# Mixer slots of a two-layer decoder trunk: other PSUM banks for the second S5 input half, and attention items spread over four column tiles

## The chip, the cores and the metric

The kernel runs as one program on 1 core of one Trainium2 chip. The metric is the device time of one execution in microseconds. Before the change it is 2696.19 us, the median of 3 runs (2693.93 to 2703.63).

## What is computed

A trunk of two layers over one sequence of 256 tokens, width 2048, all in float32. Each layer has a mixer and a gated MLP with a short causal convolution. In the mixer one projection of the normalised input feeds three groups of heads:

```
h = rmsnorm(x, g_pre_mix) * (1 + sc1) + sh1          # sh, sc, gt from silu(c) @ w_ada + b_ada
proj = h @ w_in                                      # 41 column tiles of 128 in the kernel
y_m = mlstm_group(qk, v, o, i, f)                    # gated linear attention, 2 chunks of 128
y_s = s5_group(u)                                    # complex diagonal state, scan over tokens
y_n = nsa_group(q, k_cmp, v_cmp, k_slc, v_slc, ...)  # attention of three kinds, gated sum
x = x + gt1 * rmsnorm(concat(y_m, y_s, y_n) @ w_out, g_post_mix)
```

In the attention group, for each of 2 key heads (4 query heads each), each of 2 query blocks of 128 and each of 3 kinds (compressed keys, selected blocks, window), a softmax over the keys is weighted by a gate and summed: 12 items in all. With 256 tokens every block is selected, so the second and third kind are plain causal attention over 128 or 256 keys.

## The kernel before, in words

**Split precision.** Every weight chunk (128 x 1024 f32) is loaded into one of 5 ring slots by SyncE's queue, copied to `w_hi` by ScalarE (`w_head`, L1038), and its rest is written to `w_lo` by VectorE (`w_rest`, through L1406). TensorE multiplies with both. A ring slot is loaded again when VectorE has taken the rest of the chunk in it. Small S5 and compression weights ("raw" chunks) go through the same ring and are freed by the matmuls that use them. SyncE issues the loads strictly in order.

**Column tiles.** The mixer's input projection takes 41 column tiles in the order: 4 of S5 input u (tiles 0 to 3), 12 of keys and values (4 to 15), 1 of gates (16), 8 of queries (17 to 24), 8 of mLSTM q/k (25 to 32), 4 of mLSTM v (33 to 36), 4 of mLSTM o (37 to 40). A tile is 48 matmuls (`proj`, L616) over two weight chunks. Each engine has its own loop over tiles, written by hand, in which all the smaller work of the mixer is placed at a fixed tile number:
- TensorE, tile n: `proj(n)`, then the small matmuls of that tile (`s5_in` L715, `s5_out` L730/L733, `v_tokens` L770, `scores` L803/L808, `weights_t` L825/L827, `weighted_sum` L839/L842, `reduce_unit` L590).
- ScalarE, slot n: `w_head(2n+4)`, which needs the first half of tile n done by TensorE, `in_tile(n)` (evacuates the tile), `w_head(2n+5)`, then `s5_gelu` L1178, the evacuation of `v_tokens` L1260, `weights_out` L1197/L1199, `exps` L1186, `heads_out` L1205. After a slot the next `w_head` follows.
- VectorE, slot k: `w_rest(2k+4)`, for tiles 25 to 32 the mLSTM convolution (`qk_conv`, three operations), `w_rest(2k+5)`, `masked` (scale, mask and row maximum), two or three chunks of the adaLN product in layer 0 and one or two in layer 1 (`ada_chunk`, L1412), a piece of the S5 scan in slots 19 to 24 (`s5_scan`), `weighted` (L1737 and two or three L1406).

**An attention item before.** Item j, with `ITEM_TILE` = 27: `scores(j)` on TensorE in tile 27+j; in the same slot `masked(j)` on VectorE, `exps(j)` on ScalarE, and at the end of the slot `weighted(j)` on VectorE; `weights_t(j)` (transposes) on TensorE in tile 28+j, `weights_out(j)` on ScalarE, and `weighted_sum(j)` on TensorE in tile 29+j. `scores(j)` waits for `masked(j-1)`, since all scores use PSUM banks 2 and 3. Items 4, 5, 10 and 11 have 4 x 256 scores a row, items 1, 2, 7 and 8 have 4 x 128, the others 4 x 15.

**S5 before.** Both halves of the S5 input product go to PSUM banks 2 and 3. TensorE's first matmul of the second half (tile 20) therefore waits for `s5_bv(1)`, which VectorE gives after reading the first half (`s5_scan(0, 0)`, slot 19). `s5_out(1, ...)` (tiles 25 to 27) writes bank 5, `reduce_unit` bank 7 (tiles 23, 29 and 36 in layer 0, tile 29 in layer 1).

**Gate row.** At the end of slot 33 VectorE computes the gate gain; ScalarE sends it to memory (L1077), and in slot 34 waits for it to have landed before it issues the read back (L1082). After tile 40 the mLSTM part and the output projection follow.

Of the kernel before, what the change touches and what calls it, by code (L numbers as in the profile page):

```python
# [165 lines left out]
def trunk(nc, x, c_cols, pos, consts, aux_d, ada_d, ada_b, glu_d, stream, out):  # L166
    with ExitStack() as ctx:
# [408 lines left out]
        def _(pe):  # L576
# [82 lines left out]
            for l in range(DEPTH):  # L659
# [45 lines left out]
                def s5_in(h, part):  # L705

                    n = R_IN + 2 * h + part
                    raw_full(l, n)
                    if h == 0 and part == 0:
                        s5_tr_ev.wait(pe, l, UT)  # L710
                        s5_u.wait(pe, l, 1)
                    if h == 1:
                        s5_bv.wait(pe, l, 1)
                    for j in range(SH):
                        m = pe.matmul(ps[:, 2 + part, j * SN:(j + 1) * SN], raw(n)[:, j * P:(j + 1) * P],  # L715
                                      s5_u2[:, SH * h + j, :], start=True, stop=True)
                    raw_used.by(m)

                def s5_out(h, part):
# [5 lines left out]
                    if h == 1 and part == 0:  # L725
                        ch_g.wait(pe, l, 2)
# [65 lines left out]
                def scores(n):  # L792
                    g, qt, kind = ITEMS[n]
                    if n:
                        ns_m.wait(pe, l, n)
                    else:
                        s5_bv.wait(pe, l, 2)
                        cc_ev.wait(pe, l, 2)
                        rp_d.wait(pe, l, 7)
                    for h in range(GQ):  # L800
                        q = mix[:, T_Q + GQ * g + h, qt * P:(qt + 1) * P]
                        if kind == 0:
                            m = pe.matmul(ps[:, 2, h * 16:h * 16 + NC], q, kcT[:, g * NC:(g + 1) * NC],  # L803
                                          start=True, stop=True)
                        else:
                            kt = (T_KS if kind == 1 else T_KW) + g
                            nk = (qt + 1) * P
                            m = pe.matmul(ps[:, 2 + h // 2, (h % 2) * SEQ:(h % 2) * SEQ + nk], q, mix[:, kt, 0:nk],  # L808
                                          start=True, stop=True)
                    ns_s.by(m)  # L810
# [35 lines left out]
                for n, t in enumerate(ORDER):  # L846
# [22 lines left out]
                    if n == ITEM_TILE - 2:  # L869
                        v_tokens(0)  # L870
                    if n == ITEM_TILE:
                        v_tokens(1)
                    if 0 <= n - ITEM_TILE < NI:
                        scores(n - ITEM_TILE)
                    if 0 <= n - ITEM_TILE - 1 < NI:
                        weights_t(n - ITEM_TILE - 1)
                    if 0 <= n - ITEM_TILE - 2 < NI:
                        weighted_sum(n - ITEM_TILE - 2)
                    if n in ADA_TILE[l]:
                        u = U_IN[l] + ADA_TILE[l].index(n)  # L880
                        sg_ev.wait(pe, l, 1)
# [134 lines left out]
        def _(s):  # L1016
# [13 lines left out]
            for l in range(DEPTH):  # L1030
# [177 lines left out]
                for n in range(NT):  # L1208
# [47 lines left out]
                    if n in (ITEM_TILE - 2, ITEM_TILE):  # L1256
                        a = (n - ITEM_TILE + 2) // 2
# [3 lines left out]
                    if 0 <= n - ITEM_TILE - 1 < NI:  # L1261
                        weights_out(n - ITEM_TILE - 1)
                    if 0 <= n - ITEM_TILE < NI:
                        exps(n - ITEM_TILE)
                    if n - ITEM_TILE - 2 in (2, 5, 8, 11):
                        heads_out(n - ITEM_TILE - 2)
                    if n == ITEM_TILE + 1:
# [4 lines left out]
                    if n == ITEM_TILE + 4:  # L1272
# [131 lines left out]
        def _(v):  # L1404
# [75 lines left out]
            for l in range(DEPTH):  # L1480
# [167 lines left out]
                def s5_scan(h, piece):  # L1648
# [4 lines left out]
                    re_, im_ = ps[:, 2, :], ps[:, 3, :]  # L1653
# [94 lines left out]
                for k in range(NT):  # L1748
# [3 lines left out]
                    if k < NT - 1:  # L1752
                        w_rest(2 * k + AHEAD + 1)
                    if 0 <= k - ITEM_TILE < NI:
# [25 lines left out]
                    if 0 <= k - ITEM_TILE < NI:  # L1780
                        weighted(k - ITEM_TILE)
                    if k == ITEM_TILE + 2:
# [160 lines left out]
ITEM_TILE = 27  # L1943
# [130 lines left out]
```

## Time and profile before

| | |
|---|---|
| median of 3 runs | 2696.19 us |
| profiled execution, its own time | 2703.81 us |
| its span | 2702.0 us |
| TensorE busy | 2452.4 us (91%) |
| VectorE busy | 1992.8 us (74%) |
| ScalarE busy | 1280.3 us (47%) |
| GpSimd busy | 294.2 us (11%) |

Times in the profile are us from the start of the span. Busy time of an engine is the union of its instructions; a figure in square brackets behind a row of the timeline is how long that engine had been idle before it, and for what it waited. The mixer's 41 tiles lie between about 122 and 492 us in layer 0 and between about 1436 and 1785 us in layer 1. Line numbers L1406 and L1412 are those of helpers, so the operations behind them are told apart by their tiles (`w_lo`, `ada_acc`, `mix`, `side`).

### The profile page before, as it was taken

Reading aid. Unit: us, or ns where it says so; the run is one execution under the profiler, and the core shown is the slowest. Engines: PE = TensorE matmul, PEld = TensorE weight load, DVE = VectorE, ACT = ScalarE, POOL = GpSimd, SP = SyncE. Lnnn points to the kernel's source line nnn. Section 1 sums busy time; section 2 is a strip of 40 time slices with the busy share of each in tenths; the row PEclk is TensorE's granted clock in tenths of the full one; section 3 lists DMA queues with packets and bytes.
Section 4 is the critical chain, followed back from the end, with each engine's and each line's share of the span. In section 5 each row is a group of like instructions: output and inputs, shape, how many; then the busy total and the mean of one; then the engine's idle time right before and its main releaser. Section 6 shows DMA issues by size and latency. Waiting matters only on the chain.

```text
span 2702.0 us, 41350 instructions
## 1 busy us (share of the span) xinstructions
PE 2452.4 (91%) x14516; PEld 2170.6 (80%) x14516; DVE 1992.8 (74%) x2383; ACT 1280.3 (47%) x1981; POOL 294.2 (11%) x434
## 2 busy tenths in 40 slices
PE   1499989888999999999998999987899999999998
PEld 1499878766888888878878999876788888887886
DVE  8788988677899996656666978767788666665555
ACT  1265455334544444444447446543454554554443
POOL 1031321111111110001001212001111000000000
PEclk9999899788999999999999999988899999999999
DMA  9648876566799996567763686545768555555554
GB/s 396 249 156 301 301 253 236 184 254 252 265 336 333 328 331 235 192 203 272 267 243 125 236 277 239 178 161 202 290 244 322 189 190 190 188 190 174 191 192 154
DMA packets 191466, 643.11 MB, mean 238 GB/s; under 512 B 28480, under 2 KB 36688, under 8 KB 189424
## 3 DMA queue, kind: packets, MB, share of 16 engines
q1 hardware_dynamic: 123520, 455.96, 47.8%
q0 software_dynamic: 47216, 170.80, 18.0%
q10 hardware_dynamic: 20608, 14.72, 1.7%
q8 instruction: 77, 1.26, 0.2%
q14 instruction: 45, 0.37, 0.0%
HBM read 626.68 MB, written 14.71 MB: 237 GB/s over the span
## 4 chain that ended last, share of the span: by engine, by line
PE 73%; DVE 16%; DMA 5%; ACT 3%; issue 3%; ACTq 0%; DVEq 0%; SPq 0%; POOLq 0%
PE ps L981 23%; PE ps L631 19%; PE ps L982 12%; PE ps L616 9%; DVE ada_acc L1412 5%; DVE w_lo L1406 3%; DVE mix L1406 3%; DMA ring<-stream 2%; PE ps L590 1%; PE ps L648 1%; ACT w_hi L1038 1%; PE ps L599 1%; PE ps L748 1%; DVE mix L1409 1%; DVE hT L1406 1%
## 5 line engine op out<-in xcount | busy, mean ns | idle before, releaser
L1406 DVE TENSOR_TENSOR w_lo<-ring,w_hi 128x1024 fp32r<-128x1024 f32 x744 | 917.6, 1239 | 518.8 <-ACT w_hi L1038 516.6
L1038 ACT ACTIVATE w_hi<-ring 128x1024 fp32r<-128x1024 f32 x744 | 787.5, 1059 | 978.7 <-PE ps L982 374.3
L981 PE MATMUL ps<-hT,w_hi 128*128 128x512 f32 x2752 | 958.7, 395 | 4.8 <-DVE hT L1406 4.8
L982 PE MATMUL ps<-hT,w_lo 128*128 128x256 f32 x2752 | 764.4, 278 | 0.0
L981 PEld LDWEIGHTS ps<-hT,w_hi 128*128 128x128 f32 x2752 | 516.3, 188 | 127.6 <-DVE hT L1406 5.3
L616 PE MATMUL ps<-hT,w_hi 128*128 128x256 f32 x2624 | 504.6, 294 | 28.6 <-DVE w_lo L1406 28.0
L982 PEld LDWEIGHTS ps<-hT,w_lo 128*128 128x128 f32 x2752 | 517.5, 188 | 0.0
L1412 DVE SCALAR_TENSOR_TENSOR ada_acc<-ada_w,cs,ada_acc 128x1024 f32<-128x1024 f32 x348 | 445.6, 1281 | 18.5 <-DMA ada_w<-ada_d 4.5
L616 PEld LDWEIGHTS ps<-hT,w_hi 128*128 128x128 f32 x2624 | 426.6, 200 | 39.3 <-issue 19.3
L616 PE MATMUL ps<-hT,w_lo 128*128 128x256 f32 x1312 | 380.2, 290 | 0.0
L631 PE MATMUL ps<-w_hi,x_hi 128*128 128x512 f32 x880 | 275.7, 395 | 23.1 <-DVE x_lo L1406 14.4
L631 PE MATMUL ps<-w_lo,x_hi 128*128 128x512 f32 x880 | 274.4, 393 | 0.0
L631 PE MATMUL ps<-w_hi,x_lo 128*128 128x512 f32 x880 | 273.6, 393 | 0.0
L616 PEld LDWEIGHTS ps<-hT,w_lo 128*128 128x128 f32 x1312 | 261.5, 199 | 0.0
L631 PEld LDWEIGHTS ps<-w_hi,x_hi 128*128 128x128 f32 x880 | 167.2, 191 | 62.0 <-DVE x_lo L1406 18.3
L505 POOL DMA_DIRECT2D ada_w<-ada_d x224 | 118.3, 529 | 881.7 <-DVE ada_acc L1412 859.1
L631 PEld LDWEIGHTS ps<-w_lo,x_hi 128*128 128x128 f32 x880 | 167.7, 191 | 35.3
L631 PEld LDWEIGHTS ps<-w_hi,x_lo 128*128 128x128 f32 x880 | 167.1, 190 | 35.1
L590 PE MATMUL ps<-cst,ada_acc 128*128 128x1 f32 x384 | 59.0, 285 | 106.4 <-DVE ada_acc L1412 88.7
L590 PEld LDWEIGHTS ps<-cst,ada_acc 128*128 128x128 f32 x384 | 58.8, 242 | 110.3 <-issue 90.8
L1353 ACT ACTIVATE mix<-ff_a,aux 128x256 f32 (+1 forms) x86 | 50.9, 592 | 89.6 <-DVE ff_a L1406 89.6
L1412 DVE SCALAR_TENSOR_TENSOR mix<-ff_a,aux,mix 128x255 f32 (+3 forms) x172 | 82.7, 481 | 14.5 <-DVE mix L1412 12.2
(231 smaller groups left out, 2008.6 us busy)
## 6 DMA issues: line engine op xcount, KB each, us to landing
ring<-stream SPq DMA_DIRECT2D x760, 512.0 KB, 4.4
ada_w<-ada_d POOLq DMA_DIRECT2D x320, 512.0 KB, 5.6
ring<-ada_d SPq DMA_DIRECT2D x36, 512.0 KB, 9.7
ada_w<-ada_d SPq DMA_DIRECT2D x28, 512.0 KB, 9.9
xs<-x SPq DMA_DIRECT2D x2, 2048.0 KB, 12.1
s_in_w<-mix ACTq DMA_DIRECT2D x8, 512.0 KB, 3.0
s_out_w<-mix ACTq DMA_DIRECT2D x16, 256.0 KB, 6.1
ring<-s_in_w SPq DMA_DIRECT2D x8, 512.0 KB, 5.8
```

Source lines behind the costliest of these rows:

```text
L505: pool.dma_start(ada_w[:, s, :], ada_d[bass.ds(u * UCH + j, 1), :, :].rearrange("a p n -> p (a n)")).then_inc(ada_full[s], 16)
L590: m = pe.matmul(ps[:, bank, col + k:col + k + 1], ada_acc[:, a, k * P:(k + 1) * P], ones[:, 0:1], start=True, stop=True)
L599: m = pe.matmul(ps[:, b, k * SEQ + t * P:k * SEQ + (t + 1) * P], xs[:, t, (2 * b + k) * P:(2 * b + k + 1) * P], r_diag[:, t, :], start=Tru ...
L616: m = pe.matmul(ps[:, bank, 0:SEQ], w[:, s, ks], h[:, k, :], start=k == 0 and p == 0, stop=k == KT - 1 and p == 2)
L631: m = pe.matmul(ps[:, 4 * t + 2 * half + b, :], xx[:, xs_, ts_], w[:, s, b * 512:(b + 1) * 512], start=k == 0 and p == 0, stop=False)
L648: m = pe.matmul(ps[:, 4 * t + 2 * half + b, :], xx[:, (k + j) % 2, ts_], w[:, s, b * 512:(b + 1) * 512], start=False, stop=j == 1 and p == 2)
L981: pe.matmul(ps[:, bank, :], w_hi[:, s, ks], hT[:, k, :, :], start=k == 0, stop=False)
L982: m = pe.matmul(ps[:, bank, SEQ:2 * SEQ], w_lo[:, s, ks], hT_hi[:, k, :], start=False, stop=k == KT - 1)
L1038: s.activation(w_hi[:, c % SPLIT, :], ring[:, at % RING, :], ACT.Copy).then_inc(hi_ready, 1)
L1353: s.activation(mtile(t), ff_a[:, k % 2, :], ACT.Identity, scale=w, bias=b).then_inc(ff_tap, 1)
L1406: return v.tensor_tensor(o, a, b, op)
L1412: return v.scalar_tensor_tensor(o, a, s, b, op0, op1)
```

## The change

`S5_BANK` gives the second S5 half banks 5 and 7. The first matmul of that half no longer waits for `s5_bv(1)`, but for the last readers of banks 5 and 7 before it (`ch_g(2)`, `sg_ev(1)`). `s5_out(1, 0)` and `reduce_unit`, which write those banks, now wait for `s5_bv(2)`, the end of the first four operations of `s5_scan(1, 0)` in VectorE's slot 22. `ITEM_TILE` becomes 26: `scores`, `masked` and `exps` of an item run one tile earlier; `weighted` goes from the end of slot 27+j to the place right behind the `w_rest` of the same slot, ahead of `masked(j+1)`; `weights_t` and `weighted_sum` keep their tiles. Within a tile TensorE now issues `weights_t` ahead of `scores`. `v_tokens(1)` and its evacuation go from tile 27 to 26. The mLSTM gate arithmetic keeps its slots.

```
@@ TensorE
                     if h == 1:
-                        s5_bv.wait(pe, l, 1)
+                        ch_g.wait(pe, l, 2)
+                        sg_ev.wait(pe, l, 1)
-                        m = pe.matmul(ps[:, 2 + part, ...
+                        m = pe.matmul(ps[:, S5_BANK[h][part], ...
@@ s5_out
                     if h == 1 and part == 0:
-                        ch_g.wait(pe, l, 2)
+                        s5_bv.wait(pe, l, 2)
@@ scores
-                        s5_bv.wait(pe, l, 2)
+                        s5_bv.wait(pe, l, 1)
                         cc_ev.wait(pe, l, 2)
+                        rp_d.wait(pe, l, 5)
+                    if n == NI // 2:
                         rp_d.wait(pe, l, 7)
@@ TensorE's tile loop
-                    if n == ITEM_TILE - 2:
-                        v_tokens(0)
-                    if n == ITEM_TILE:
-                        v_tokens(1)
+                    if n in V_TILES:
+                        v_tokens(V_TILES.index(n))
+                    if 0 <= n - ITEM_TILE - 2 < NI:
+                        weights_t(n - ITEM_TILE - 2)
                     if 0 <= n - ITEM_TILE < NI:
                         scores(n - ITEM_TILE)
-                    if 0 <= n - ITEM_TILE - 1 < NI:
-                        weights_t(n - ITEM_TILE - 1)
-                    if 0 <= n - ITEM_TILE - 2 < NI:
-                        weighted_sum(n - ITEM_TILE - 2)
+                    if 0 <= n - ITEM_TILE - 3 < NI:
+                        weighted_sum(n - ITEM_TILE - 3)
                     if n in ADA_TILE[l]:
-                        sg_ev.wait(pe, l, 1)
+                        s5_bv.wait(pe, l, 2)
                         reduce_unit(u, u % 2, u)
@@ ScalarE's tile loop
-                    if 0 <= n - ITEM_TILE - 1 < NI:
-                        weights_out(n - ITEM_TILE - 1)
+                    if 0 <= n - ITEM_TILE - 2 < NI:
+                        weights_out(n - ITEM_TILE - 2)
                     if 0 <= n - ITEM_TILE < NI:
                         exps(n - ITEM_TILE)
-                    if n - ITEM_TILE - 2 in (2, 5, 8, 11):
-                        heads_out(n - ITEM_TILE - 2)
+                    if n - ITEM_TILE - 3 in (2, 5, 8, 11):
+                        heads_out(n - ITEM_TILE - 3)
@@ VectorE
-                    re_, im_ = ps[:, 2, :], ps[:, 3, :]
+                    re_, im_ = (ps[:, b, :] for b in S5_BANK[h])
...
+                    if 0 <= k - ITEM_TILE - 1 < NI:
+                        weighted(k - ITEM_TILE - 1)
                     if 0 <= k - ITEM_TILE < NI:
                         masked(k - ITEM_TILE)
...
-                    if 0 <= k - ITEM_TILE < NI:
-                        weighted(k - ITEM_TILE)
@@ constants
-ITEM_TILE = 27
+S5_BANK = ((2, 3), (5, 7))
+ITEM_TILE = 26
+V_TILES = (25, 26)
```

## Rows read from the trace of the kernel before

**Rows 1.** The page, part 4: the chain that ended last, by engine.
```profile
PE 73%; DVE 16%; DMA 5%; ACT 3%; issue 3%; ACTq 0%; DVEq 0%; SPq 0%; POOLq 0%
```

**Rows 2.** Windows by stage: stretch, its length, busy us by engine, clock, DMA share, GB/s.
```profile
255.00:346.20 91.20, 83.08 (x669) 81.89 (x667) 84.03 (x74) 39.16 (x70) 31.45 (x36) 0.93 0.81 293
373.10:434.60 61.50, 55.27 (x369) 48.60 (x370) 56.16 (x86) 32.01 (x79) 8.87 (x16) 0.91 0.66 216
434.60:492.40 57.80, 57.12 (x423) 51.49 (x422) 47.97 (x56) 34.51 (x73) 9.39 (x17) 1.00 0.71 247
1672.80:1729.60 56.80, 53.70 (x370) 48.04 (x371) 47.60 (x79) 31.89 (x79) 3.69 (x7) 0.93 0.55 175
```

**Rows 3.** Waits, layer 0, 255 to 495 us: total us, times, longest.
```profile
DVE w_lo L1406 <- ACT w_hi L1038: 15.3, 13, 2.9
PE ps L825 <- DVE side L1406: 9.8, 2, 7.0
DVE att_s L1737 <- ACT side L1186: 5.4, 2, 3.9
PE ps L827 <- DVE side L1406: 3.3, 3, 1.4
```

**Rows 4.** Waits, layer 1, 1575 to 1790 us.
```profile
DVE w_lo L1406 <- ACT w_hi L1038: 28.6, 15, 4.7
DVE att_s L1737 <- ACT side L1186: 13.2, 9, 5.4
PE ps L825 <- DVE side L1406: 5.6, 3, 5.0
PE ps L827 <- DVE side L1406: 3.1, 3, 1.8
```

**Rows 5.** Timeline of TensorE: S5 second half (tile 20) and the first reduction (tile 23).
```profile
291.43 3.65 PE L715 MATMUL ps<-mix,ring 128*128 128x64 f32 x16 [6.50 <-DVE mix L1406]
319.85 1.90 PE L590 MATMUL ps<-cst,ada_acc 128*128 128x1 f32 x16
```

**Rows 6.** Timeline of VectorE around the S5 scan, layer 0, then slot 21 of layer 1.
```profile
288.41 2.87 DVE L1406 TENSOR_TENSOR mix<-ps,mix 128x512 f32<-128x512 f32 x4 [2.53 <-DMA s_own_w<-mix]
305.38 1.22 DVE L1406 TENSOR_TENSOR w_lo<-ring,w_hi 128x1024 fp32r<-128x1024 f32 x1 [0.76 <-ACT w_hi L1038]
319.39 2.86 DVE L1406 TENSOR_TENSOR mix<-ps,mix 128x512 f32<-128x512 f32 x4
1614.65 1.22 DVE L1406 TENSOR_TENSOR w_lo<-ring,w_hi 128x1024 fp32r<-128x1024 f32 x1 [2.08 <-ACT w_hi L1038]
```

**Rows 7.** Timeline of VectorE, slot 31 of layer 0 from item 4's mask on.
```profile
408.52 1.22 DVE L1412 SCALAR_TENSOR_TENSOR side<-ps,cst 128x1024 f32<-128x1024 f32 x1
410.91 2.66 DVE L1412 SCALAR_TENSOR_TENSOR ada_acc<-ada_w,cs,ada_acc 128x1024 f32<-128x1024 f32 x2
413.90 1.23 DVE L1406 TENSOR_TENSOR side<-side,att_s 128x1024 f32<-128x1024 f32 x1
415.16 1.23 DVE L1406 TENSOR_TENSOR w_lo<-ring,w_hi 128x1024 fp32r<-128x1024 f32 x1
```

**Rows 8.** Timeline of ScalarE, layer 0: table load, exp, head of slot 32.
```profile
369.58 1.28 ACT L1186 ACT_TABLE_LOAD   x1
370.87 0.31 ACT L1186 ACTIVATE side<-side,att_s 128x15 f32<-128x15 f32 x1
414.09 1.04 ACT L1038 ACTIVATE w_hi<-ring 128x1024 fp32r<-128x1024 f32 x1
```

**Rows 9.** Timelines of ScalarE and VectorE: gate row and end of the ring.
```profile
434.61 0.37 ACTq L1077 DMA_DIRECT2D gate_rows<-gg  x1
445.03 0.34 ACTq L1082 DMA_DIRECT2D mix<-gate_rows  x1
473.09 2.35 DVE L1406 TENSOR_TENSOR w_lo<-ring,w_hi 128x1024 fp32r<-128x1024 f32 x2
483.34 1.06 ACT L1038 ACTIVATE w_hi<-ring 128x1024 fp32r<-128x1024 f32 x1 [2.91 <-DMA ring<-stream]
```

More of the change, by code:

```diff
@@ L712, in s5_in @@
                     if h == 1:
-                        s5_bv.wait(pe, l, 1)
+                        ch_g.wait(pe, l, 2)
+                        sg_ev.wait(pe, l, 1)
                     for j in range(SH):
-                        m = pe.matmul(ps[:, 2 + part, j * SN:(j + 1) * SN], raw(n)[:, j * P:(j + 1) * P],
+                        m = pe.matmul(ps[:, S5_BANK[h][part], j * SN:(j + 1) * SN], raw(n)[:, j * P:(j + 1) * P],
                                       s5_u2[:, SH * h + j, :], start=True, stop=True)
@@ L1255, in _ @@
                         s5_gelu((n - OUT_TILE) // 3)
-                    if n in (ITEM_TILE - 2, ITEM_TILE):
-                        a = (n - ITEM_TILE + 2) // 2
+                    if n in V_TILES:
+                        a = V_TILES.index(n)
                         vt_mm.wait(s, l, a + 1)
@@ L1260, in _ @@
                         vt_ev.by(s.activation(vtok[:, a, :, :, :].rearrange("p h s e -> p (h s e)"), ps[:, 4, :], ACT.Copy))
-                    if 0 <= n - ITEM_TILE - 1 < NI:
-                        weights_out(n - ITEM_TILE - 1)
+                    if 0 <= n - ITEM_TILE - 2 < NI:
+                        weights_out(n - ITEM_TILE - 2)
                     if 0 <= n - ITEM_TILE < NI:
                         exps(n - ITEM_TILE)
-                    if n - ITEM_TILE - 2 in (2, 5, 8, 11):
-                        heads_out(n - ITEM_TILE - 2)
-                    if n == ITEM_TILE + 1:
+                    if n - ITEM_TILE - 3 in (2, 5, 8, 11):
+                        heads_out(n - ITEM_TILE - 3)
+                    if n == ITEM_TILE + 2:
                         gate_ev.wait(s, l, 2)
@@ L1271, in _ @@
                         mg_a.by(s.activation(rows(2), rows(2), ACT.Ln, bias=1.0))
-                    if n == ITEM_TILE + 4:
+                    if n == ITEM_TILE + 5:
                         mg_d.wait(s, l, 2)
@@ L1779, in _ @@
                         ada_finish(u, mod_col(u))
-                    if 0 <= k - ITEM_TILE < NI:
-                        weighted(k - ITEM_TILE)
-                    if k == ITEM_TILE + 2:
+                    if k == ITEM_TILE + 3:
                         gate_chain()
```

## The prediction, made before the changed kernel ran

> **What bounds the kernel now.** I read the chain of waits first. By engine it is TensorE for 73% and VectorE for 16% [rows 1]; the change touches only the mixers, so I went on to busy time by stage. In the S5 stretch of layer 0 (255 to 346 us) VectorE works 84.03 of 91.20 us, TensorE 83.08; in the first part of the attention items (373.1 to 434.6) VectorE 56.16 of 61.50, TensorE 55.27; in the last part TensorE 57.12 of 57.80, VectorE 47.97 [rows 2]. In layer 1's first part TensorE has 53.70 of 56.80, VectorE 47.60 [rows 2]. So where TensorE waits in layer 0, VectorE is the engine without slack, and TensorE's waits are its shadow. The list of waits says the same from the other side. TensorE's transposes wait for `weighted` 9.8 and 3.3 us in layer 0 [rows 3], 5.6 and 3.1 us in layer 1 [rows 4]: 21.8 us in all. Tile 20 waits 6.50 us for the first S5 half [rows 5]. These are the waits that the change takes away. But VectorE has its own: 5.4 and 13.2 us for `exps` and 15.3 and 28.6 us for `w_hi`, both from ScalarE [rows 3, 4]. Only what shortens VectorE's and ScalarE's common round, or comes where TensorE alone is the limit, shortens the run.
>
> **S5 half in other banks, layer 0.** Removed: 6.50 us at tile 20, and some 2 us behind it while the clock was low (a group of 16 small matmuls took 3.65 us after the idle time, 1.90 for the 16 of the reduction, not an equal group but the nearest row) [rows 5]. VectorE doesn't move: its first four operations start at 288.41, released by a DMA of S5 weights, not by TensorE [rows 6], and from there to 346 us it hardly pauses; one pause of 0.76 us for `w_hi` at 305.38 is due to TensorE's delay [rows 6] and goes. What is late next is a wait that the change adds. The reduction in tile 23 writes bank 7, now read by the second scan half, so it waits for that half's four reads, 319.39 plus 2.86 = 322.25 in slot 22 [rows 6], less the 0.76 won: 321.5. It started at 319.85 before [rows 5]. TensorE, some 9 us ahead, stands there until 321.5, with tile 24 and all later tiles queued behind it: 1.6 us later than before, where a few us of slack await `s5_h(2)` in tile 26. Gain 0 to 0.8 us; I take 0.8 for VectorE.
>
> **The same in layer 1.** There is no reduction in tile 23 there. VectorE's pause of 2.08 us for `w_hi` in slot 21 [rows 6] is of TensorE's making and goes: VectorE and TensorE reach tile 26 some 2.4 us earlier (that pause, and a shorter one before it).
>
> **Items one tile earlier: the beginning.** `exps(0)` now lies between the two gelus of S5 in ScalarE's queue. The exp needs a table load of 1.28 us [rows 8], the second gelu needs the old table again, `exps(1)` the new one: 3 loads for 1. The first is hidden, since ScalarE waits for `masked(0)` anyway; two of 1.28 us stand in the path from `w_hi(59)` over the gelu and `exps(1)` to `w_hi(60)`. Against them: the 0.60 us evacuation is already done, the pull of the paragraphs above, and `exps(1)` is 0.4 longer than `exps(0)`. By the steps: VectorE's slot 28 starts +0.5 us in layer 0, -1.2 us in layer 1.
> The Trainium skill, page "ScalarE: Activation LUTs", section "What ACT_TABLE_LOAD costs", speaks against this order: a switch is a load of about 1283 ns and about 1380 ns of drain. Here the load took 1.28 us and the exp began at 370.87, at its end [rows 8], so no drain shows behind it and 2 x 1.28 is the trace's price; by the page the two switches would cost 5.3 us a layer in place of 2.6.
> TensorE's longest wait, 7.0 us in tile 28 [rows 3], is gone, as `weighted(0)` is long done. But tile 29 asks for `weighted(1)`, which needs `w_rest(60)`, the convolution and `w_rest(61)` first: slot 28 start plus 3.7 plus 1.1, some 378.4, with TensorE there at 373. So 5 of the 7 us reappear one tile later.
>
> **The steady slots.** What a slot costs with four rows of 256 keys, from layer 0's slot 31: the two `w_rest` and the convolution 3.7 us (four operations' starts), mask and maximum from 408.52 to 410.91 = 2.4, two ada chunks 2.66, the weighting with its small operations 1.56 (the large one is 1.23 from 413.90) [rows 7]. After the maximum ScalarE does `exps`, `heads_out` and the gate rows, begins `w_hi` at 414.09 and ends it at 415.13 [rows 8]: 4.2 us. VectorE meanwhile does ada and the weighting and goes on at 415.16 [rows 7]: covered, but exactly. After the change the weighting stands ahead of the mask, so only ada covers those 4.2 us: 2.66 against 4.2 leaves 1.5 us open. In slots with three chunks (4.05 us) or without the extras (ScalarE's path is then 3.1) it is 0 to 0.5, in layer 1 with one chunk (1.28) 1.8, where before VectorE waited 13.2 us over 9 slots for `exps`, 1.5 a slot [rows 4], so 0.3 more.
> Added up for VectorE in layer 0, where each slot also holds the mask of one item later (a heavy one 1 us or more dearer than the one it replaces): slot 30 starts at +0.8 (396.8), slot 31 at +3.0, slot 32 at +4.4 (419.6 for 415.16), slot 34 at +1.9 (light masks fall due earlier, too). Layer 1: slot 31 +2.1, slot 32 +3.8, slot 34 0.
> For TensorE it is better than that, because it now waits for the middle of a VectorE slot, not its end: though slot 32 ends 2.5 us later, `weighted(5)` in it is done 1.9 us earlier. So TensorE starts tile 34 some 1.5 us earlier in layer 0, with one score group more done (1.06 us); 1.6 us in layer 1.
>
> **The end of the mixer.** The gate row is a fixed round: sent at 434.61, landed and reread at 445.03, 10.4 us, with ScalarE held [rows 9]. Its start is the end of VectorE's slot 33: +1.9 in layer 0, 0 in layer 1. From there items 10 and 11, heavy ones, have masks and exps a slot earlier, ahead of `w_hi(80)`: the rest of chunk 81, done at 475.44 before [rows 9], comes at 480.0. It frees the ring for the next loads; SyncE's queue is in order, and the first of them landed by 483.34, 7.9 us later [rows 9]: now 487.9. Queued behind this `w_hi(82)` on ScalarE are two evacuations, `w_hi(83)` and `weights_out(11)`, 3.5 us: 491.4, and TensorE's last weighted sum waits for it. Its own tiles are done at 490.6 (before, 492.4, and no wait). So the lead of 1.8 us shrinks to 0.8, and the first operation of the mLSTM part on VectorE comes 0.4 later, its queue being late. Layer 0: -0.8 to +0.4. Layer 1 by the same steps: load at 1781.8 for 1777.8, last weighted sum +0.3.
>
> **Sum.** -0.2 for layer 0 and +0.3 for layer 1: nothing. For the profiled execution 2703.8 us (span 2702.0); the median of the runs shown is 7.6 us lower, and the difference of nothing goes onto the median: 2696 us. Unknown costs: the contention of VectorE with GpSimd's ropes, which may shift against each other (I allow 4 us a layer, either sign, an estimate from GpSimd's 31.45 us of work in the S5 stretch [rows 2], of which little can move), and whether the low clock after an idle time falls on other tiles (1.5 us each, either sign, one or two a layer).
>
> **The rivals.**
> (B) VectorE's waits for `exps`, 5.4 + 13.2 = 18.6 us [rows 3, 4], vanish, as a weighting now comes a slot after its exp, and do not come back as waits for `w_hi`: 2677.5 us. For: they do vanish, and in layer 1 VectorE has slack. Against: `exps` and `w_hi` stand behind each other on ScalarE, so the wait moves from one to the other, as in slot 31.
> (C) TensorE's waits are real delays and go: 21.8 + 6.5 = 28.3 us, 2667.9. Against: VectorE's 56.16 of 61.50 us [rows 2] has 5.3 us to give in the stretch.
> (D) Slower. ScalarE's path from the maximum to the next `w_hi` decides every slot: from the point where it (3.1 to 4.2 us) exceeds the slot's ada work (1.28 to 4.05). If TensorE's lead gives none of it back, it costs 8 heavy slots x 1.3 = 10.4 and the four table loads 5.1 us, less the 3.2 of the S5 part: 12.3, 2708.5 us. For: layer 1's one-chunk slots. Against: in the last part TensorE, not this round, is the limit [rows 2].
> (A) The forecast, nothing: 2696, own range 2688 to 2702.
> That the banks' half doesn't do what it says in layer 0 is in (A): its wait returns in tile 23.
>
> **How the numbers follow.** (A) 0.78, (B) 0.12, (C) 0.04, (D) 0.06. About 0.5%, 13.5 us, is what a measurement of this kernel tells from no change (its three runs span 9.7 us). Faster by more: nearly all of (B) and (C), 0.14; slower by more: half of (D) and a little of (A)'s doubt, 0.04; the rest 0.82. The range leaves out (C) and half of (B) below and most of (D) above: 2680 to 2705.
>
> **What would show it.** Right: tile 20 without a wait; TensorE waiting some us ahead of L590 in tile 23 of layer 0 only; three table loads between the first S5 gelu and item 1's exp; no wait in tile 28 and one of about 5 us in tile 29; VectorE's waits for L1186 near nothing and for `w_hi` larger by about as much; gate row of layer 0 sent 435 to 437 us from the start; the first output chunk waited for longer than 2.91 us or later than 483.3. Wrong: the gate row sent before 431 us, or the mixers' tile 40 ending over 4 us earlier in a layer.

## The result, and the profile after

| kernel | median | runs |
|---|---|---|
| before | 2699.45 us (2693.93 to 2706.36) | 9 |
| after | 2708.81 us (2705.17 to 2714.36) | 9 |

The ratio is 1.0037, 95% interval 1.0022 to 1.0051: about 10 us slower (6 to 14). The forecast was no change, 2696 us, range 2680 to 2705; the time lies above it. In the kernel after, the lines of TensorE's small matmuls are some 3 higher than before: `weights_t` L828/L830, `weighted_sum` L842/L845, `scores` L806/L811; on ScalarE `w_hi` is L1039, `exps` L1187, `heads_out` L1206, and `w_lo` on VectorE is L1407.

The profiled run of after took 2708.81 us (span 2707.0), that of before 2703.81. The chain of work that ended last, by engine, which answers to [rows 1]:

```profile
PE 70%; DVE 19%; DMA 4%; ACT 4%; issue 3%; DVEq 0%; ACTq 0%; SPq 0%; POOLq 0%
```

TensorE's share fell by 3 points and VectorE's rose by 3: more of the chain now runs through VectorE's work. Next the waits of after in layer 0, 255 to 499 us (engine, tile, line, what it waited for: us in total, times, longest), which answer to [rows 3]:

```profile
DVE w_lo L1407 <- ACT w_hi L1039: 31.3, 13, 4.6
...
PE ps L830 <- DVE side L1407: 6.9, 2, 6.3
PE ps L842 <- ACT mix L1206: 5.0, 2, 3.4
PE ps L590 <- DVE mix L1407: 3.9, 1, 3.9
PE ps L734 <- DVE mix L1407: 2.8, 1, 2.8
```

and in layer 1, 1574 to 1795 us, for [rows 4]:

```profile
DVE w_lo L1407 <- ACT w_hi L1039: 48.2, 18, 6.1
...
PE ps L830 <- DVE side L1407: 5.3, 1, 5.3
PE ps L842 <- ACT mix L1206: 3.9, 2, 2.7
PE ps L811 <- DVE att_s L1727: 1.2, 1, 1.2
```

Three things are to be seen. VectorE's waits for `exps` (5.4 and 13.2 us before) have left the list, and those for `w_hi` grew from 15.3 to 31.3 and from 28.6 to 48.2. TensorE's waits for `weighted` went from 13.1 to 6.9 and from 8.7 to 5.3. And there is a row that no view of before has and that the prediction didn't have either: **TensorE's `weighted_sum` (L842) waits for `heads_out` (L1206)**, 5.0 us in layer 0 and 3.9 in layer 1. (L590 is new as well, but was forecast; of the small new rows none is over 1.5 us.)

The windows of after (stretch, its length, busy us of PE, PEld, DVE, ACT, POOL with counts, PE clock, DMA share, GB/s) show the same place; the first two and the third answer to the last three of [rows 2]:

```profile
379.45:437.20 57.75, 53.98 (x330) 47.65 (x331) 51.34 (x78) 30.15 (x76) 8.35 (x15) 0.84 0.64 208
437.20:498.70 61.50, 57.85 (x405) 51.13 (x404) 46.01 (x53) 32.32 (x66) 8.88 (x16) 0.97 0.78 235
1675.20:1728.50 53.30, 51.87 (x312) 45.98 (x313) 42.52 (x71) 29.92 (x75) 3.17 (x6) 0.81 0.49 160
```

In the last part of layer 0 TensorE was busy for 57.12 of 57.80 us before; now it has 3.65 us of idle time in 61.50 and a clock of 0.97 in place of 1.00. In the earlier part the clock is 0.84 where it was 0.91, in layer 1's 0.81 where it was 0.93.

Measured from tile 18 (2.1 us behind the end of its projection, when its first small matmuls are done) to the end of the last weighted sum, the two mixers took 224.7 and 203.3 us before and 228.1 and 209.5 us after: +3.4 and +6.2, 9.6 us together. The medians differ by 9.4, but these two profiled executions by 5.0 only, so the rest of the span went the other way by 4.6. The split between the layers is of one profile each and scatters too: a second profile of after (`after_again`) has 230.9 and 207.5.

### The profile page after: what moved, and what is told of

Its sections match the earlier page's. It is cut to its first block, busy times and chain, and to the rows that moved or that the text cites. A ratio compares the mean times of both kernels' runs of the same rounds, so it can differ in the third digit from the quotient of the medians.

```text
span 2707.0 us, 41356 instructions
## 1 busy us (share of the span) xinstructions
PE 2456.1 (91%) x14516; PEld 2175.1 (80%) x14516; DVE 1989.1 (73%) x2383; ACT 1285.8 (47%) x1985; POOL 293.8 (11%) x434
## 4 chain that ended last, share of the span: by engine, by line
PE 70%; DVE 19%; DMA 4%; ACT 4%; issue 3%; DVEq 0%; ACTq 0%; SPq 0%; POOLq 0%
PE ps L982 23%; PE ps L631 19%; PE ps L983 12%; PE ps L616 8%; DVE ada_acc L1413 5%; DVE w_lo L1407 4%; DVE mix L1407 3%; DMA ring<-stream 2%; PE ps L590 1%; PE ps L648 1%; ACT w_hi L1039 1%; PE ps L599 1%; DVE mix L1410 1%; PE ps L749 1%; DVE mix L1413 1%
## 5 line engine op out<-in xcount | busy, mean ns | idle before, releaser
L1407 DVE TENSOR_TENSOR w_lo<-ring,w_hi 128x1024 fp32r<-128x1024 f32 x744 | 915.3, 1236 | 551.5 <-ACT w_hi L1039 549.7
L1039 ACT ACTIVATE w_hi<-ring 128x1024 fp32r<-128x1024 f32 x744 | 787.4, 1059 | 988.0 <-PE ps L983 371.8
L631 PE MATMUL ps<-w_hi,x_hi 128*128 128x512 f32 x880 | 274.3, 393 | 25.3 <-DVE x_lo L1407 16.6
L505 POOL DMA_DIRECT2D ada_w<-ada_d x224 | 118.3, 529 | 874.8 <-DVE ada_acc L1413 852.3
L590 PE MATMUL ps<-cst,ada_acc 128*128 128x1 f32 x384 | 64.7, 299 | 110.3 <-DVE ada_acc L1413 88.6
L590 PEld LDWEIGHTS ps<-cst,ada_acc 128*128 128x128 f32 x384 | 64.5, 262 | 115.8 <-issue 92.3
L549 POOL DMA_DIRECT2D ada_w<-ada_d x96 | 51.4, 535 | 398.5 <-DVE ada_acc L1413 398.5
```

The lines of the kernel that those rows point to most:

```text
L505: pool.dma_start(ada_w[:, s, :], ada_d[bass.ds(u * UCH + j, 1), :, :].rearrange("a p n -> p (a n)")).then_inc(ada_full[s], 16)
L549: pool.dma_start(ada_w[:, j % ASLOT, :], ada_d[u * UCH + j % UCH, :, :]).then_inc(ada_full[j % ASLOT], 16)
L590: m = pe.matmul(ps[:, bank, col + k:col + k + 1], ada_acc[:, a, k * P:(k + 1) * P], ones[:, 0:1], start=True, stop=True)
L631: m = pe.matmul(ps[:, 4 * t + 2 * half + b, :], xx[:, xs_, ts_], w[:, s, b * 512:(b + 1) * 512], start=k == 0 and p == 0, stop=False)
L1039: s.activation(w_hi[:, c % SPLIT, :], ring[:, at % RING, :], ACT.Copy).then_inc(hi_ready, 1)
L1407: return v.tensor_tensor(o, a, b, op)
```

## How the missed wait comes about

Each group of three items (one key head, one query block) is summed up in PSUM bank 6. `heads_out(2)` empties it into `mix` on ScalarE, and only then may `weighted_sum(3)`, the first of the next group, write it; the same holds for items 8 and 9. Both kernels run `heads_out(2)` in ScalarE's slot 31, `weighted_sum(3)` in TensorE's tile 32, and ScalarE's `exps` of that slot ahead of `heads_out`. But before, this is `exps(4)`, and `heads_out` was done 2.6 us (416.20 less 413.58) before TensorE began the sum. Layer 0, kernel before:

```profile
411.03 0.51 ACT L1186 ACTIVATE side<-side,att_s 128x256 f32<-128x256 f32 x1 [3.91 <-DVE att_s L1726]
...
413.01 0.57 ACT L1205 ACTIVATE mix<-ps 128x512 f32<-128x512 f32 x1
416.20 1.12 PE L839 MATMUL ps<-side,cmp_s 15*128 15x512 f32 x2
```

In the changed kernel it is `exps(5)`, for which VectorE must first do two `w_rest` and the convolution, then `weighted(4)`, then the mask and maximum of item 5. VectorE in slot 31 of layer 0, kernel after:

```profile
412.07 0.17 DVE L1738 RECIPROCAL att_s<-att_s 128x4 f32<-128x4 f32 x1
...
412.47 1.23 DVE L1407 TENSOR_TENSOR side<-side,att_s 128x1024 f32<-128x1024 f32 x1
413.61 1.22 DVE L1413 SCALAR_TENSOR_TENSOR side<-ps,cst 128x1024 f32<-128x1024 f32 x1
414.86 1.22 DVE L1727 TENSOR_REDUCE att_s<-side 128x4 f32<-128x1024 f32 x1
```

ScalarE, same slot:

```profile
416.11 0.51 ACT L1187 ACTIVATE side<-side,att_s 128x256 f32<-128x256 f32 x1 [6.77 <-DVE att_s L1727]
...
418.10 0.57 ACT L1206 ACTIVATE mix<-ps 128x512 f32<-128x512 f32 x1
```

and TensorE in tiles 32 and 38 of layer 0, then of layer 1:

```profile
418.82 2.02 PE L842 MATMUL ps<-side,cmp_s 15*128 15x512 f32 x2 [1.62 <-ACT mix L1206]
479.28 1.09 PE L842 MATMUL ps<-side,cmp_s 15*128 15x512 f32 x2 [3.39 <-ACT mix L1206]
1712.32 1.88 PE L842 MATMUL ps<-side,cmp_s 15*128 15x512 f32 x2 [1.22 <-ACT mix L1206]
1771.16 2.04 PE L842 MATMUL ps<-side,cmp_s 15*128 15x512 f32 x2 [2.67 <-ACT mix L1206]
```

ScalarE stood idle for 6.77 us for the maximum of item 5, with an evacuation of 0.57 us queued behind that needed nothing from VectorE; `heads_out` came at 418.10, 5.1 us later than before. Of these 1.2 us lie ahead of the changed part, since tile 18 of this profile ended at 268.51, before at 267.31. The four waits are 1.62 + 3.39 + 1.22 + 2.67 = 8.9 us. Behind them TensorE's clock is lower: the projections of tiles 33 and 39 took 8.1 and 7.1 us in layer 0 and 8.3 and 7.5 in layer 1; before, 7.5, 6.0, 6.0 and 6.0. That is 5.5 us more, and 14.4 with the waits; TensorE's shorter waits for `weighted` pay some of it back. In layer 0 not all of the 5.5 belongs to this wait: ahead of it in tile 32 `scores` waits 1.29 us for the maximum of item 5, and heads_first, below, has the slow tiles of layer 0 without the wait.

## The experiments

Ratios are to the kernel before, run on the same chip beside each. Its median was between 2699.5 and 2704.6 us each time.

### Which half of the change

**after_again**: the changed kernel once more.

> The changed kernel once more, on the chip of the runs beside it. Both theories expect about 9 us over the kernel before (ratio 1.0035), since nothing is changed.

Measured: 1.0045 (1.0022 to 1.0068), 2717.44 us. The loss is there again, nominally larger than expected and within the interval.

**s5_only**: the kernel before with the banks' half alone.

```
+S5_BANK = ((2, 3), (5, 7))
-                        s5_bv.wait(pe, l, 1)
+                        ch_g.wait(pe, l, 2)
+                        sg_ev.wait(pe, l, 1)
```

> The kernel before with the banks' half of the change alone (second S5 half in banks 5 and 7, the reduction and s5_out waiting for the second half's reads; items as before). Theory 1 (the loss is made by the items): -1 to -3 us against the kernel before, nearly all in layer 1; in layer 0 tile 20 no longer waits and tile 23 does, for about 4 us, and its reduction runs at the low clock. Rival (the new wait in tile 23 with its clock makes a good part of the loss): +2 to +4 us.

Measured: 0.9988 (0.9968 to 1.0009), 2700.38 us. Its mixers took 222.9 and 198.1 us in the trace, but the interval includes no change. TensorE's waits in layer 0:

```profile
PE ps L826 <- DVE side L1407: 10.5, 2, 7.7
PE ps L828 <- DVE side L1407: 4.1, 3, 2.8
PE ps L590 <- DVE mix L1407: 3.9, 1, 3.9
PE ps L734 <- DVE mix L1407: 2.9, 1, 2.9
```

The 6.50 us of tile 20 came back as 3.9 + 2.9 in tile 23, the first of them predicted.

**items_only**: the changed kernel with both S5 halves in banks 2 and 3, as before.

```
-S5_BANK = ((2, 3), (5, 7))
+S5_BANK = ((2, 3), (2, 3))
```

> The changed kernel with the S5 half back in banks 2 and 3 and its old waits; only the items are moved. Theory 1 (the items make the loss): +9 to +12 us against the kernel before, with TensorE waiting some 9 us in all for heads_out in four tiles. Rival (the banks' half makes it): +3 to +5 us.

Measured: 1.0045 (1.0023 to 1.0067), 2714.36 us. With s5_only this puts the whole loss, as far as it can be measured, on the items. The waits for `heads_out` are there, 5.0 and 4.2 us.

### Taking the wait away, in two ways

**heads_first**: the changed kernel with the evacuation ahead of `exps` in ScalarE's queue.

```
+                    if n - ITEM_TILE - 3 in (2, 5, 8, 11):
+                        heads_out(n - ITEM_TILE - 3)
                     if 0 <= n - ITEM_TILE < NI:
                         exps(n - ITEM_TILE)
-                    if n - ITEM_TILE - 3 in (2, 5, 8, 11):
-                        heads_out(n - ITEM_TILE - 3)
```

> The changed kernel with heads_out ahead of exps in ScalarE's slot. Theory 1 (weighted_sum of items 3 and 9 waits for the heads_out that stands behind the exps of items 5 and 11, and the low clock follows): the four waits of 1.6, 3.4, 1.2 and 2.7 us go and the tiles behind them take 6.0 us again in place of 7.2 to 8.3; of these 16 us some 5 to 9 come off the time, to 0 to +4 us against the kernel before. Rival (ScalarE's and VectorE's common round is the limit, the TensorE wait only its shadow): the time stays at +7 to +10 us, and TensorE waits elsewhere.

Measured: 0.9999 (0.9978 to 1.0019), 2705.0 us. The 10 us are back, at the better end of what was expected. TensorE in tile 32 of layer 0:

```profile
418.00 1.77 PE L842 MATMUL ps<-side,cmp_s 15*128 15x512 f32 x2
```

No idle time ahead of it. The windows around the waits at tile 38 of layer 0, tile 32 and tile 38 of layer 1, of heads_first:

```profile
476.00:494.00 18.00, 15.61 (x103) 13.63 (x102) 12.34 (x13) 7.63 (x16) 2.64 (x5) 0.91 0.75 270
1708.00:1725.00 17.00, 16.55 (x124) 14.61 (x123) 14.12 (x20) 9.25 (x25) 1.28 (x3) 1.00 0.44 140
1766.00:1788.00 22.00, 22.00 (x160) 19.10 (x158) 14.22 (x17) 10.60 (x21) 2.54 (x4) 1.00 0.54 190
```

and of after:

```profile
476.00:494.00 18.00, 14.72 (x95) 12.99 (x96) 12.04 (x14) 8.57 (x18) 2.64 (x5) 0.91 0.75 267
1708.00:1725.00 17.00, 15.78 (x97) 13.74 (x97) 13.08 (x18) 9.95 (x26) 1.58 (x3) 0.80 0.43 137
1766.00:1788.00 22.00, 19.33 (x123) 16.61 (x122) 12.36 (x13) 10.77 (x20) 3.07 (x5) 0.84 0.49 173
```

In layer 1 the clock goes from 0.80 and 0.84 to 1.00. TensorE gets through 124 and 160 matmul records in place of 97 and 123, but not of the same part of the work: layer 1 began 3.0 us later in this profile. By tiles, the projections of 33 and 39 in layer 1 took 6.0 and 6.0 us in place of 8.3 and 7.5, and the mixer 203.1 us (after, 209.5), as before. In layer 0 little moved: 8.4 and 7.2 us for the two projections, 227.5 for 228.1 us in all. There, with the wait of 3.39 us gone from tile 38, a wait of 2.4 us for `mod` on VectorE stands a few matmuls later in the same tile (`m_tokens`, L783), and the 1.3 us of `scores` in tile 32 are still there. VectorE's waits for `w_hi` stayed, 28.3 and 45.5 us.

**mask_first**: the changed kernel with VectorE's `masked` ahead of `weighted`, so that the maximum, `exps` and with it `heads_out` come sooner.

```
-                    if 0 <= k - ITEM_TILE - 1 < NI:
-                        weighted(k - ITEM_TILE - 1)
                     if 0 <= k - ITEM_TILE < NI:
                         masked(k - ITEM_TILE)
+                    if 0 <= k - ITEM_TILE - 1 < NI:
+                        weighted(k - ITEM_TILE - 1)
```

> The changed kernel with masked ahead of weighted in VectorE's slot, so that exps starts up to 1.6 us earlier and more of ScalarE's path from the maximum to the next w_hi is covered. Theory 2 (this round decides the slots): -3 to -6 us against the changed kernel, heads_out earlier too. Rival (only the place of heads_out in ScalarE's queue counts): the waits for heads_out shrink by up to 1.6 us each, weights_t waits up to 2.4 us more, and the time moves less than 2 us.

Measured: 0.9998 (0.9980 to 1.0017), 2701.22 us. `heads_out` began at 416.35 in slot 31 (after, 418.10), and no wait for it is left in either layer. TensorE's waits in layer 1:

```profile
PE ps L830 <- DVE side L1407: 6.5, 1, 6.5
PE ps L828 <- DVE side L1407: 1.0, 1, 1.0
PE ps L734 <- DVE mix L1407: 0.9, 1, 0.9
```

Two edits on two engines, one that puts `exps` behind the evacuation and one that brings both forward, recover the same time. Neither expectation had this: theory 2 had 3 to 6 us for the edit, the rival less than 2, and 10 to 13 us came off the changed kernel. The waits for `heads_out` went wholly, not by 1.6 us each. The edit is not a clean one, for it moves other waits as well: VectorE's for `w_hi` are 26.3 and 44.5 us, though hardly less than in heads_first, and in layer 0 TensorE's for `weighted` rose from 6.9 to 11.5 and its last weighted sum waits 2.4 us for ScalarE.

### The table loads

**after_copy** and **before_copy**: the kernel after and the kernel before with a plain copy for the gelu of the second S5 output half, which is left out.

```
-  ... ACT.Gelu_apprx_tanh)
+  ... ACT.Copy if h else ACT.Gelu_apprx_tanh)
```

> The changed kernel with the gelu of the second S5 half replaced by a copy (that gelu is left out), which needs no table: of the three table loads from the first gelu to item 1's exp one is left. To be read against before_copy. Theory 3 (the added loads, 2.6 us a layer, are on the path): the changed kernel gains 3 to 5 us by this edit, the kernel before nothing. Rival (they are covered): under 1.5 us.

> The kernel before with the same gelu replaced by a copy (that gelu is left out). All theories: within 1.5 us of the kernel before, as only the table load ahead of item 0's exp is left in both.

Measured: 1.0003 (0.9987 to 1.0019), 2705.49 us, and 0.9991 (0.9975 to 1.0006), 2701.54 us. So this, too, makes up for the loss, by more than the 3 to 5 us expected, and it doesn't do so by removing the missed wait. TensorE in tiles 29, 32 and 38 of layer 0, then 29 of layer 1:

```profile
376.76 0.66 PE L830 MATMUL ps<-cst,side 128*128 128x128 f32 x4 [3.61 <-DVE side L1407]
416.12 2.04 PE L842 MATMUL ps<-side,cmp_s 15*128 15x512 f32 x2 [1.62 <-ACT mix L1206]
478.56 1.09 PE L842 MATMUL ps<-side,cmp_s 15*128 15x512 f32 x2 [3.38 <-ACT mix L1206]
1677.37 0.66 PE L830 MATMUL ps<-cst,side 128*128 128x128 f32 x4 [1.81 <-DVE side L1407]
```

The waits for `heads_out` stand; what shrank is the wait in tile 29, from 6.28 to 3.61 and from 5.35 to 1.81, 6.2 us together, since two loads less stand ahead of `exps(1)`. (The copies take as long as the gelu did, 6.53 and 6.51 us.)

**gelu28**: the changed kernel with the second gelu moved, not left out: to ScalarE's slot 28, behind `weights_out(0)`.

```
-                    if n in (OUT_TILE + 2, OUT_TILE + 5):
-                        s5_gelu((n - OUT_TILE) // 3)
+                    if n == OUT_TILE + 2:
+                        s5_gelu(0)
...
+                    if n == OUT_TILE + 6:
+                        s5_gelu(1)
```

> The changed kernel with the gelu of the second S5 half in slot 28, behind weights_out(0), in place of slot 27: the 6.5 us and the table loads no longer stand between item 0's exp and w_hi(60), but in a slot where ScalarE waits 4.2 us for a mask. Theory 3 (the gelu with its loads on the path at slot 27 sets the head of the item stretch, and by it everything up to the gate row): TensorE's wait of 6.3 us in tile 29 goes or halves and the time falls by 4 to 8 us against the changed kernel. Rival (the loss is made by heads_out in tiles 32 and 38 alone): under 2 us, and these waits are as before.

Measured: 1.0048 (1.0030 to 1.0066), 2713.49 us. Nothing won. The wait in tile 29 fell to 1.78 us in layer 0 and TensorE reached tile 30 at 111.9 us from tile 18, counted as for the mixers, in place of 117.5, but it reached tile 32 at 135.4 for 136.2: tile 31 took 12.6 us for 8.7. Layer 1 is alike (94.4 for 101.4, then 118.2 for 120.8, with 12.0 us for tile 31 where it was 8.8). Time won ahead of `weighted(2)` is given back there. The waits for `heads_out` stand (0.79 and 3.22 us in layer 0, 4.3 in layer 1), nearly as in after, and nothing came off the time: the expectation's rival holds, its theory of 4 to 8 us doesn't.

**copy_heads**: after_copy with heads_first's order, the gelu left out as there.

> The changed kernel with heads_out ahead of exps on ScalarE and, as in after_copy, the second gelu of the S5 output left out (a plain copy in its place). Theory A (the gelu's table loads and the late evacuations are two ways to the same lost time around tiles 28 to 32, and only one of them can be had): within 2 us of heads_first and after_copy, that is of before. Theory B (they are two separate losses of some 8 us each): about 8 us faster than before.

Measured: 0.9992 (0.9977 to 1.0006), 2701.62 us. The two recoveries don't add up: each alone gives the 10 us back, both together measure 2 to 3 us less than that, within the intervals. The trace of layer 1 shows a next limit, and the kernel before doesn't have it: in copy_heads as in heads_first `scores` waits 1.8 us in tile 37 for the maximum (L811), where before the list has none for it in layer 1. No run isolates what that wait costs.

### The other new wait, and all together

**heads_red3**: heads_first with the reduction of tile 23 in bank 3, so that it needn't wait for the second S5 half's reads. **s5_red3**: s5_only with the same.

```
-                        s5_bv.wait(pe, l, 2)
-                        reduce_unit(u, u % 2, u)
+                        s5_bv.wait(pe, l, 1 if n < ITEM_TILE else 2)
+                        reduce_unit(u, u % 2, u, 3 if n < ITEM_TILE else 7)
```

> heads_first with the reduction of tile 23 in bank 3, which is free there, waiting for the first S5 half's reads only. Theory 1: the wait of 3.9 us in tile 23 goes and its 16 matmuls take 1.9 us in place of 3.6, but layer 0 gains under 2 us, since VectorE has no slack up to tile 26. Rival (TensorE's lead counts): 4 us or more off heads_first.

> The banks' half alone, with the reduction of tile 23 in bank 3 so that it adds no wait. Theory 1 (VectorE has no slack in layer 0 up to tile 26): within 2 us of the banks' half alone, so -2 to -5 us against the kernel before; TensorE's wait moves from tile 23 to tiles 26 to 28. Rival (TensorE's lead counts): -6 us or more.

Measured: 0.9996 (0.9981 to 1.0011), 2702.48 us; 1.0006 (0.9990 to 1.0022), 2700.47 us beside 2700.15. The wait of L590 in tile 23 costs nothing that can be measured: without it TensorE waits in tiles 26 to 28 (2.4 us in heads_red3). s5_red3 was expected 2 to 5 us below the kernel before and measured 1.6 us above it, within 4.

**all3** (heads_first, mask_first and bank 3 together) and **all4** (with gelu28 too):

> Changed kernel with heads_out ahead of exps, masked ahead of weighted and the reduction of tile 23 in bank 3. If the three causes are separate, their gains (10.6, 10.0 and about 1 us against the changed kernel) would add to some -20 us, 10 below the kernel before; if heads_first and mask_first remove the same waits (the exps that stand ahead of heads_out come earlier or go behind it), it is -11 to -14, so 0 to -4 us against the kernel before. I expect the second.

> all3 with the second gelu in slot 28. Theory 3: 3 to 6 us below all3, so -4 to -10 us against the kernel before. Rival (the gelu delays something in slot 28 as much as it did in slot 27): within 2 us of all3.

Measured: 1.0003 (0.9988 to 1.0017), 2701.18 us; 1.0005 (0.9989 to 1.0021), 2701.36 us. all3 was expected 0 to 4 us below the kernel before; all4 lies within 2 us of all3, as its rival said. No version of the change is measurably faster than the kernel before.

### Putting the wait alone into the kernel before

**heads_late** and **heads_late32**: the kernel before; `heads_out(2)` and `heads_out(8)` go to slots 32 and 38, behind the second `w_hi` of the slot, cut into 8 or 32 pieces so that they take longer.

```
-                    if n - ITEM_TILE - 2 in (2, 5, 8, 11):
+                    if n - ITEM_TILE - 2 in (5, 11):
...
+                    if n - ITEM_TILE - 3 in (2, 8):
+                        heads_out(n - ITEM_TILE - 3, 32)
                     if 0 <= n - ITEM_TILE - 1 < NI:
                         weights_out(n - ITEM_TILE - 1)
```

> The kernel before with one thing changed: the evacuations heads_out(2) and heads_out(8) stand one slot later in ScalarE's order (slots 32 and 38, behind w_hi(69) and w_hi(81)) and are cut into 8 pieces, some 2 us together, so that weighted_sum(3) and weighted_sum(9) have to wait for PSUM bank 6. Nothing of the change is in it. Theory (a wait of TensorE for L1205 in those two tiles of each layer goes into the time, with the low clock behind it): two waits of about 2 to 3 us a layer appear on weighted_sum, the time grows by 5 to 12 us. Rival (such a wait lies in time that TensorE has to give away later anyway, and the loss of the changed kernel is from elsewhere): the waits appear, and the time is within 2 us of before.

> As heads_late (the kernel before, with the evacuations heads_out(2) and heads_out(8) one slot later), but cut into 32 pieces in place of 8: eight pieces took only 0.92 us and left one wait of 0.7 and one of 1.1 us, at 1.0016 of the time of before. 32 pieces should take about 3 to 4 us and make four waits of 2 to 3.5 us before weighted_sum(3) and weighted_sum(9), about as large as those of the changed kernel. Theory (the wait for the evacuation is what the changed kernel lost): 8 to 14 us slower than before, ratio 1.003 to 1.005. Rival (such a wait is made up for later): within 2 us of heads_late or of before.

Eight pieces took only 0.92 to 1.02 us and left one wait a layer, 0.7 and 1.1 us; measured 1.0016 (1.0000 to 1.0033). The dose was too small to tell the theories apart. With 32 pieces TensorE had, in tiles 32 and 38 of both layers:

```profile
417.98 1.56 PE L839 MATMUL ps<-side,cmp_s 15*128 15x512 f32 x2 [2.04 <-ACT mix L1212]
478.88 1.09 PE L839 MATMUL ps<-side,cmp_s 15*128 15x512 f32 x2 [1.35 <-ACT mix L1212]
1713.55 2.04 PE L839 MATMUL ps<-side,cmp_s 15*128 15x512 f32 x2 [2.51 <-ACT mix L1212]
1769.99 1.09 PE L839 MATMUL ps<-side,cmp_s 15*128 15x512 f32 x2 [1.35 <-ACT mix L1212]
```

7.25 us in all, and the kernel took 1.0028 (1.0010 to 1.0046) of the time of before, 7.6 us more. The ratio is just under the 1.003 to 1.005 expected, and its interval leaves out 1. A rival remains: 32 pieces also hold ScalarE 2 us longer, and what is queued behind them comes later. VectorE's waits for ScalarE speak against much of that: for `w_hi` and `exps` together they are 24.6 and 41.1 us, before 20.7 and 41.8. Side by side:

| kernel | waits for `heads_out`, both layers | against before |
|---|---|---|
| heads_first, mask_first | 0 | -0.3 and -0.5 us (each within 6) |
| heads_late | 1.8 us | +4.3 us (0 to 9) |
| heads_late32 | 7.25 us | +7.6 us (3 to 12) |
| after_copy | 8.1 us | +0.8 us (-4 to +5) |
| gelu28 | 8.3 us | +13.0 us (8 to 18) |
| after | 8.9 us | +10.0 us (6 to 14) |
| items_only | 9.2 us | +12.2 us (6 to 18) |

Without the wait no kernel is measurably slower than before. With 7 us or more of it all are but after_copy, and the trace shows why that is no contradiction. Take the last three tiles, from TensorE's start of tile 38 to the end of the last weighted sum, and what lies ahead of them:

| kernel | start of tile 38 against before, layers 0 and 1 | from there to the end, layers 0 and 1 |
|---|---|---|
| before | 0, 0 | 27.7, 26.8 us |
| after | +1.1, +2.4 us | 30.0, 30.6 us |
| after_copy | +0.3, -3.9 us | 30.0, 30.5 us |
| heads_first | +1.4, +1.3 us | 29.1, 25.3 us |
| mask_first | -1.3, -1.7 us | 31.9, 25.2 us |
| heads_late32 | +1.6, -1.1 us | 29.7, 28.2 us |

Starts are counted from the end of tile 18's projection. In layer 1 this end takes 29.3 to 30.7 us in every changed kernel that has the wait (after, after_again, items_only, gelu28, after_copy) and 25.1 to 25.3 in each of the six that haven't: the wait of tile 38 with the low clock behind it costs 4 to 6 us there. after_copy pays that in full and has won 6.3 us ahead of it. In layer 0 the end is no shorter without the wait, because others take its place: 2.4 us for `mod` in heads_first, 2.4 us for ScalarE in mask_first. And ahead of tile 38, where the first of the two waits lies, after is only 1.1 and 2.4 us late.

So the wait is shown from both sides: taken out of the changed kernel, the loss goes; put into the kernel before, a loss of 3 to 12 us comes. How much each microsecond of it costs is not shown: in the traces the wait of tile 38 in layer 1 stands in the time, that of tile 32 is in the main given back, and heads_late32's two mixers are 3.9 us longer than before's, not 7.6.

## Why the prediction was wrong, point by point

**The step that failed** is in "The end of the mixer": "Its own tiles are done at 490.6 (before, 492.4, and no wait)". Measured, layer 0's last tile was done at 497.0: counted from tile 18, 3.4 us later than before in place of 1.8 earlier. Layer 1's last weighted sum, put at +0.3, came at +6.2. TensorE's tiles were taken to run without a wait from tile 34 on, and slot 32's weighting was counted as its only condition in tiles 32 and 33. The condition on bank 6 was not among those gone through. It was in the code (`ns_y` ahead of the first weighted sum of a group), and the prediction had both numbers for it, without putting them together: "slot 31 at +3.0" on VectorE, and the weighting put ahead of the mask. A later maximum makes a later `exps`, and `heads_out` stands behind it. From its own rows, 3.0 plus 1.56 us for the weighting put `heads_out` some 4.6 us later (an estimate), against 2.6 us to spare. The working names `heads_out` in ScalarE's path behind the maximum, but follows that path only to the next `w_hi`, not to TensorE.

**The lead of TensorE** failed with it: tile 34 was to start 1.5 us earlier in layer 0 and 1.6 in layer 1. Counted from tile 18 it started 0.3 and 1.1 us later.

**The base.** Of the 12.6 us between the forecast and 2708.81, 3.3 are not of the change: the median of before was 2696.19 over three runs and 2699.45 over nine. Without that the time would still lie just above the range: 1.0037 times 2696.19 is 2706.2.

**Right.** Tile 20 is without a wait for the first half. TensorE waits ahead of L590 in tile 23 of layer 0 only, and tile 29 has most of the wait that tile 28 lost (about 5 us predicted; 6.28 and 5.35):

```profile
320.92 3.57 PE L590 MATMUL ps<-cst,ada_acc 128*128 128x1 f32 x16 [3.89 <-DVE mix L1407]
379.45 1.12 PE L830 MATMUL ps<-cst,side 128*128 128x128 f32 x4 [6.28 <-DVE side L1407]
1675.19 1.11 PE L830 MATMUL ps<-cst,side 128*128 128x128 f32 x4 [5.35 <-DVE side L1407]
```

Three table loads lie between the first gelu and item 1's exp, and the exp follows the last at once:

```profile
352.22 1.28 ACT L1187 ACT_TABLE_LOAD   x1
362.84 1.28 ACT L1179 ACT_TABLE_LOAD   x1
370.67 1.28 ACT L1187 ACT_TABLE_LOAD   x1
371.97 0.40 ACT L1187 ACTIVATE side<-side,att_s 128x128 f32<-128x128 f32 x1
```

The Trainium skill, page "ScalarE: Activation LUTs", section "What ACT_TABLE_LOAD costs", adds a drain of about 1380 ns to each. Here the exp starts 1.30 us after the load began, and the load 0.02 us after the last gelu ended, so that drain is again not seen. VectorE's waits for `exps` turned into waits for `w_hi`: 18.6 us gone, 35.6 come. Slot 31's head on VectorE and the gate row are within 1 us: sent at 437.02, predicted 436.5 (with the 1.2 us that this profile was late at tile 18).

**Sizes.** The waits for `w_hi` grew by nearly twice what was priced. The round of the gate row was taken as fixed at 10.4 us and took 12.75:

```profile
437.02 0.37 ACTq L1078 DMA_DIRECT2D gate_rows<-gg  x1
449.77 0.34 ACTq L1083 DMA_DIRECT2D mix<-gate_rows  x1
490.70 1.06 ACT L1039 ACTIVATE w_hi<-ring 128x1024 fp32r<-128x1024 f32 x1 [8.01 <-DMA ring<-stream]
```

so that `w_hi(82)` came at 490.70, not 487.9; TensorE was later still, so neither decided. The low clock was priced at "1.5 us each, either sign, one or two a layer"; the 16 matmuls of L590 in tile 23 took 3.57 us behind the wait in place of 1.90 [rows 5], and in the two layers tiles 33 and 39 together took 5.5 us more, all with the same sign. The allowance of 4 us a layer for VectorE beside GpSimd was not tested.

**The rivals.** (B) and (C) fell with the result. (D) said 2708.5, and the time was 2708.8, but that is luck, not its mechanism: heads_first keeps 28.3 and 45.5 of the 31.3 and 48.2 us that VectorE waits for `w_hi`, and takes the time of before. ScalarE's path from the maximum decides when `heads_out` runs, and TensorE waits for that; the slot as a whole didn't set the time. Its term for the table loads, 5.1 us, stays open: leaving two loads a layer out (after_copy) gave some 9 us, moving the gelu with them (gelu28) gave nothing.

**Open.** How the 10 us split. In the traces the mixers of after are 9.6 us longer than before's: 6.1 from tile 38 on, 3.5 ahead of it, where the wait of tile 32, the low clock behind the moved wait of tile 29 and the waits for the maximum lie together. after_copy recovers its 10 us mostly ahead of tile 38 in layer 1 (6.3 us), more there than the 3.5 us of the shorter wait in tile 29; no run separates the rest. And why the banks' half, some 5 us shorter in layer 1's trace, isn't measurably faster in the timed runs.

## What to carry to other kernels

When work is moved ahead in one engine's queue, go through everything behind it in that queue up to the same slot's end, and for each ask who waits for it: here a PSUM evacuation of 0.57 us that needed nothing new stood behind an exp that now waited 6.77 us. Evacuations that free a bank go ahead of instructions that wait for another engine. And a new row in the list of waits of a pair that was not in it before is worth more than a change in size of old rows: VectorE's waits for `w_hi` grew by 35.6 us here, and heads_first kept most of that at the time of before; the 8.9 us of the new row made the loss.

## What was not expected of the hardware

An evacuation of 128x512 took 0.57 us, 8 pieces of 128x64 took 0.92 to 1.02 us and 32 pieces of 128x16 took 2.33 to 2.54 us, all from PSUM. Back to back that is some 0.12 and 0.07 us a piece, though one piece of 128x16 by itself is recorded at 0.16 us or more: consecutive pieces overlap. And the write of the gate row to memory, from sending to the end of ScalarE's wait for its landing, took 10.4 us before and 12.75 after in layer 0, 12.4 and 13.9 in layer 1: such a transfer's time isn't a constant.
